# Seven block products in place of eight for the experts' down projection, with the weight sums made on VectorE

## The reference

```python
def expert_block(args):
    xb, e = args
    h = xb @ gu_w[e] + gu_b[e]
    x_glu = jnp.minimum(h[:, 0::2], SWIGLU_LIMIT)
    x_lin = jnp.clip(h[:, 1::2], -SWIGLU_LIMIT, SWIGLU_LIMIT)
    act = x_glu * jax.nn.sigmoid(SWIGLU_ALPHA * x_glu) * (x_lin + 1.0)
    return act @ dn_w[e] + dn_b[e]
```

## Time and profile before

| | |
|---|---|
| median of 3 runs | 2276.58 us (2274.15 to 2279.27) |
| the profiled execution, its own time | 2280.95 us |
| its span on the chip | 2279.3 us |
| PE busy | 2226.0 us, 98% of the span |
| DVE / ACT / POOL busy | 781.6 / 473.7 / 343.5 us |
| L2063 (gate and up), share of the chain that ended last | 39% |
| L2083 (down halves), the same | 19% |

### The profile page before, as it was taken

The page is one execution under the profiler, slowest core; times in us unless marked ns, Lnnn a source line. Parts: engine busy times, 40 slices in busy tenths (PEclk is TensorE's granted clock), DMA queues, the critical chain, the costliest instruction groups (busy, mean ns, idle before and its releaser), DMA issues.

```text
span 2279.3 us, 46156 instructions
## 1 busy us (share of the span) xinstructions
PE 2226.0 (98%) x18230; PEld 1644.5 (72%) x18231; DVE 781.6 (34%) x1853; ACT 473.7 (21%) x988; POOL 343.5 (15%) x360
## 2 busy tenths in 40 slices
PE   8999998899999999999999999999999999999997
PEld 3444445888445778887788878788778887788875
DVE  6465543455434222222222222232222232223224
ACT  3232001444333111111211111111111111111113
POOL 0000001121022212111121211122111121121112
PEclk9999999999998999999999999999999999999998
DMA  3111112334433767977777977789777988678877
GB/s 142 60 50 46 55 55 63 96 104 132 174 138 103 310 253 298 332 307 300 293 301 291 350 300 269 260 335 348 300 276 277 333 348 308 253 295 331 347 295 260
DMA packets 111411, 534.99 MB, mean 235 GB/s; under 512 B 26771, under 2 KB 60711, under 8 KB 86752
## 3 DMA queue, kind: packets, MB, share of 16 engines
q1 hardware_dynamic: 89200, 489.30, 55.2%
q0 software_dynamic: 22160, 44.98, 7.8%
HBM read 485.24 MB, written 40.05 MB: 230 GB/s over the span
## 4 chain that ended last, share of the span: by engine, by line
PE 95%; DMA 2%; DVE 1%; issue 1%; POOL 0%; ACT 0%; SPq 0%; POOLq 0%; DVEq 0%
PE ps L2063 39%; PE ps L2083 19%; PE ps L1571 9%; PE ps L1669 5%; PE ps L1942 5%; PE ps L2093 2%; PE ps L2072 2%; PE ps L1768 2%; PE ps L1618 1%; PE ps L1777 1%; PE ps L2102 1%; PE ps L1750 1%; DMA idx_g<-list_s 1%; PE ps L1782 1%; PE ps L1870 1%
## 5 line engine op out<-in xcount | busy, mean ns | idle before, releaser
L2063 PEld LDWEIGHTS ps<-arena 128*128 128x128 f32 x7808 | 925.9, 191 | 16.6 <-issue 15.1
L2063 PE MATMUL ps<-arena 128*128 128x128 f32 (+2 forms) x7808 | 926.9, 281 | 1.3 <-ACT arena L995 1.3
L2083 PE MATMUL ps<-arena 128*128 128x512 f32 x1024 | 454.3, 596 | 0.0
L2083 PEld LDWEIGHTS ps<-arena 128*128 128x128 f32 x1024 | 190.7, 190 | 221.8 <-issue 221.1
L1468 DVE TENSOR_SCALAR arena<-ps,arena 128x160 f32<-128x160 f32 x256 | 98.2, 384 | 620.1 <-PE ps L2063 536.1
L1000 ACT ACTIVATE arena<-arena 128x160 f32<-128x160 f32 x256 | 86.1, 336 | 828.3 <-DVE arena L1468 828.3
L1571 PE MATMUL ps<-arena 128*128 128x512 f32 x448 | 195.7, 594 | 0.0
L703 POOL DMA_INDIRECT sum_s<-arena,idx_s x31 | 51.5, 1663 | 824.6 <-ACT arena L1015 824.6
L1571 PEld LDWEIGHTS ps<-arena 128*128 128x128 f32 x448 | 84.5, 190 | 109.4 <-issue 109.4
L1669 PE MATMUL ps<-arena 128*128 128x512 f32 x280 | 120.6, 592 | 0.8 <-ACT arena L844 0.8
L1942 PE MATMUL ps<-arena 128*128 128x512 f32 x256 | 113.7, 594 | 0.0
(11 more groups left out here) (271 smaller groups left out, 1965.5 us busy)
## 6 DMA issues: line engine op xcount, KB each, us to landing
arena<-gu_w SPq DMA_DIRECT2D x128, 2048.0 KB, 11.7
arena<-dn_w SPq DMA_DIRECT2D x64, 2048.0 KB, 14.6
arena<-dn_b SPq DMA_DIRECT2D x32, 512.0 KB, 16.2
arena<-w_in_t SPq DMA_DIRECT2D x26, 512.0 KB, 3.2
arena<-arena SPq DMA_DIRECT2D x50, 256.0 KB, 2.7
arena<-w_out SPq DMA_DIRECT2D x2, 2048.0 KB, 8.4
arena<-x SPq DMA_DIRECT2D x8, 512.0 KB, 5.2
xn_s<-arena SPq DMA_DIRECT2D x8, 512.0 KB, 2.7
```

Source lines behind the costliest of these rows:

```text
L2063: last = nc.tensor.matmul(ps[:, f % 2, k * C:k * C + size], wslot[u][:, kt, o:o + P], xT[:, kt, 0:size], start=kt == 0, stop=kt == KT - 1, ...
L2083: last = nc.tensor.matmul(ps[:, 2 + h, :], actT[:, ft, 0:P], wslot[4 + h][:, ft, :], start=ft == 0, stop=ft == KT - 1)
```

## The change

The 128 tokens are split into two halves of 64 rows, `lower` and `upper` (as stationary operands, and as PSUM partitions), and the 1024 input features into two halves (features 0 to 3 and 4 to 7 of `actT`), so `act` becomes a11, a12 (lower rows), a21, a22 (upper rows). The weights become d11, d12 (first input half) and d21, d22. Seven products of 64 x 512 by 512 x 512 stand for the eight. `both` issues two of them side by side: one with 64 columns of the array and PSUM partitions 0 to 63, the other with the other 64. The seventh is cut into two column quarters that go side by side. DVE makes four weight sums (each 128 x 2048, in two instructions of 128 x 1024) between the steps of `glu`, and five sums of activations. DVE also puts the results together, with 64 row adds from PSUM. The down product of the last expert keeps the old form, in code of its own behind the loop. The down weights come in four loads of 1 MB, in the order of their use, at the same point of the loop as before. ACT scales the result rows in another order, at the end. The sums of rows at the end of the kernel are loaded to slots at 0 to 32 KB instead of at 112 and 56. One semaphore pair in the convolution is merged: L1271 now waits for both copies instead of one.

```diff
+                sp.dma_start(d12, down_of(e, 0, 1)).then_inc(s_wd1, 16)
+                sp.dma_start(d11, down_of(e, 0, 0)).then_inc(s_wd1, 16)
+                sp.dma_start(d22, down_of(e, 1, 1)).then_inc(s_wd22, 16)
+                sp.dma_start(d21, down_of(e, 1, 0)).then_inc(s_wd21, 16)
...
+            def down_sum(dst, a, b, op, h):
+                w = slice(h * K2 // 2, (h + 1) * K2 // 2)
+                nc.vector.tensor_tensor(dst[:, w, :], a[:, w, :], b[:, w, :], op).then_inc(s_ds, 1)
+
+            def down_sums(n, q, f):
+                if f == 2:
+                    dve.wait_ge(s_wd1, 32 * n + 32)
+                    for h in range(2):
+                        down_sum(d_dif, d12, d11, ALU.subtract, h)
+                if f in (3, 4):
+                    dve.wait_ge(s_wd22, 16 * n + 16)
+                    down_sum(d12, d12, d22, ALU.subtract, f - 3)
+                if f in (4, 5):
+                    dve.wait_ge(s_ds, 8 * q + 8 + f - 3)
+                    down_sum(d_mix, d22, d_dif, ALU.subtract, f - 4)
+                if f == 6:
+                    dve.wait_ge(s_wd21, 16 * n + 16)
+                    for h in range(2):
+                        dve.wait_ge(s_ds, 8 * q + 8 + 5 + h)
+                        down_sum(d_all, d21, d_mix, ALU.subtract, h)
...
                     for f in range(KT):
                         glu(n, e, f)
+                        down_sums(n, q, f)
+                        if f == K2:
+                            dve.wait_ge(s_act, 8 * n + KT + K2)
+                            act_sum(q, a_low, a21, a11, ALU.subtract, 0)
+                    dve.wait_ge(s_act, 8 * n + KT + KT)
+                    act_sum(q, a_sum, a21, a22, ALU.add, 1)
+                    act_sum(q, a_dif, a_sum, a11, ALU.subtract, 2)
+                    dve.wait_ge(s_db, 16 * (PIECES + 1) * (n + 1))
+                    dve.wait_ge(s_dn, o + 1)
+                    nc.vector.tensor_tensor(y_first[upper], ps[lower, 2, :], dnb[lower, 0:HALF], ALU.add).then_inc(s_ye, 1)
+                    act_sum(q, a_rest, actT[:, 0:K2, P:C], actT[:, K2:KT, P:C], ALU.add, 0)
+                    act_sum(q, a_all, a12, a_dif, ALU.subtract, 3)
                     dve.wait_ge(s_scr, n + 1)
...
+                    dve.wait_ge(s_dn, o + 2)
+                    nc.vector.tensor_tensor(Yt[upper, 0:HALF], ps[lower, 2, :], dnb[lower, 0:HALF], ALU.add).then_inc(s_ye, 1)
...
+            def both(low, high, done):
+
+                for k in range(K2):
+                    for rows, (bank, acts, weights, first) in ((lower, low), (upper, high)):
+                        width = weights.shape[-1]
+                        last = nc.tensor.matmul(ps[rows, bank, 0:width], acts[:, k, :], weights[:, k, :],
+                                                start=first and k == 0, stop=k == K2 - 1, skip_group_check=True)
+                if done:
+                    last.then_inc(s_dn, 1)
...
+            def down_first(n, q, o):
+                pe.wait_ge(s_wd1, 32 * n + 32)
+                pe.wait_ge(s_as, 5 * q + 5 + 1)
+                pe.wait_ge(s_ds, 8 * q + 8 + 4)
+                pe.wait_ge(s_ye, o + 5)
+                both((2, a11, d11, True), (3, a_low, d12, True), True)
+
+            def down_second(n, q, o):
+                pe.wait_ge(s_as, 5 * q + 5 + 3)
+                pe.wait_ge(s_ds, 8 * q + 8 + 6)
+                pe.wait_ge(s_wd21, 16 * n + 16)
+                pe.wait_ge(s_ye, o + 6)
+                both((2, a_dif, d_mix, False), (2, a12, d21, True), True)
+
+            def down_third(n, m, q, o):
+                pe.wait_ge(s_ds, 8 * q + 8 + 8)
+                pe.wait_ge(s_xe, 3 * m + 4)
+                pe.wait_ge(s_ye, o + 7)
+                both((2, a_sum, d_dif, False), (4, a22, d_all, True), True)
+                pe.wait_ge(s_as, 5 * q + 5 + 5)
+                pe.wait_ge(s_ye, o + 8)
+                both((6, a_all, d22[:, :, 0:PW], True), (6, a_all, d22[:, :, PW:HALF], True), True)
...
                     with pe.If(turn > 0):
-                        down_half(n, 0)
+                        down_first(n, q, o)
                     size = size_at(turn)
-                    transpose_tokens(m)
+                    transpose_tokens(m, 0)
+                    with pe.If(turn > 0):
+                        down_second(n, q, o)
+                    transpose_tokens(m, 1)
                     with pe.If(size > 1):
-                        down_rest(n)
+                        down_rest(n, o, q)
...
                     with pe.If(turn > 0):
-                        down_half(n, 1)
+                        down_third(n, m, q, o)
```

More of the change, by code:

```diff
@@ L241, in build @@
         wslot = [at(o, KT, HALF) for o in (0, 16, 32, 64, 80, 96)]
+        K2, TH = KT // 2, P // 2
+        d11, d21 = wslot[4][:, 0:K2, :], wslot[4][:, K2:KT, :]
+        d12, d22 = wslot[5][:, 0:K2, :], wslot[5][:, K2:KT, :]
+        d_dif, d_mix, d_all = (at(o, K2, HALF) for o in (112, 120, 128))
+        a_sum, a_dif, a_low, a_all = (at(56 + k, K2, TH) for k in range(4))
+        a_rest = at(60, K2, REST)
+        y_first, y_both = at(61, HALF), at(53, HALF)
         xg = at(48, D)
@@ L258, in build @@
         GROUPS = TT // GROUP
-        sums = [at(112 + 8 * g, GROUP, D) if g < 3 else at(56, GROUP, D) for g in range(GROUPS)]
+        sums = [at(8 * g, GROUP, D) for g in range(GROUPS)]
         rows, rows2 = at(178, D), at(182, PW)
@@ L609, in _ @@
                 pool.sem_inc(ahead, by)
-            for ahead, by in ((s_ye, 6), (s_xe, 3), (s_gd, KT), (s_act, KT)):
+            for ahead, by in ((s_ye, 5), (s_xe, 3), (s_gd, KT), (s_act, KT), (s_as, 5), (s_ds, 8)):
                 pool.sem_inc(ahead, by)
@@ new lines, in down_third, with transpose_tokens @@
+            def down_third(n, m, q, o):
[6 more added lines that the diff above has]
+                both((6, a_all, d22[:, :, 0:PW], True), (6, a_all, d22[:, :, PW:HALF], True), True)
+            def transpose_tokens(m, part):
+                if part == 0:
+                    pe.wait_ge(s_gx, 16 * m + 16)
+                for kt in range(4 * part, 4 * part + 4):
@@ L2111, in expert_pe @@
+                if part == 1:
+                    pe.wait_ge(s_gx2, 16 * m + 16)
+                    for k in range(2):
+                        last = nc.tensor.transpose(ps[:, 7, k * P:(k + 1) * P], xg2[:, k * P:(k + 1) * P], ident)
+                    last.then_inc(s_xt, 1)
             def expert_pe(r):
@@ L2141, in expert_pe @@
                         gate_up_end()
+                if isinstance(r, int):
+                    n, m = E - 1, E
+                    size = size_at(E)
+                    down_half(n, 0)
+                    for part in range(2):
+                        transpose_tokens(m, part)
+                    with pe.If(size > 1):
+                        down_rest(n, 5 * n)
+                    with pe.If(size == 1):
+                        no_rest(5 * n)
+                    down_half(n, 1)
                 if isinstance(r, int):
```

145 lines of the change are left out of this document (88 added, 57 removed).

## The result

The changed kernel took 2648.32 us (median of 4, 2644.44 to 2653.18) against 2276.18 us for the kernel before (2274.15 to 2279.27): a ratio of 1.1635 [1.1609, 1.166], 372 us slower. The forecast was 2258 us, with a range up to 2277. It was wrong by a mechanism that none of its cases held.

The account below looks back on a forecast made before the run. The prediction took PE's matmuls to bound the experts' stage. 31 turns at 0.69 us gain 21.4 us, less 3 us for first passes, is 18.4; from the median 2276.6 that gives 2258 us, range 2243 to 2277.

Parts of the forecast that it names:

- Code that runs for the first time does cost: On PE, three first passes where there were two and a separate last expert: 3 us once, bounds 0 and 8.
- Full overlap of pairs: Down product: two 64-column products run side by side, eight pairs in 3.43 us; 12.0 us a turn instead of 13.74.
- the rival of incomplete pairs: Down product: pairs overlap only partly; a quarter longer costs 93 us less the 18, about 2351 us. Chance 0.05.
- Changes of shape: PE's down part: each change of array tile shape costs 0.09 us; seven a turn where there were two.
- the load behind: PE's first weight load after a change of shape isn't hidden: 0.10 us for 128 columns, half that for 64.
- `y_first`: DVE's read of the first down product, awaited by PE before the second: 0.23 us of new waiting a turn.
- The down part: PE's down stretch of a turn: 17.93 us against 18.62 with a rest, 14.51 against 15.20 without; 0.69 us gained.
- Weight sums: DVE's eight adds of 1024 elements between `glu` steps, 1.22 us each, 9.8 us an expert: cost PE nothing.
- late DVE: Rival: DVE falls behind if an add takes 1.5 us; 0.45 us a turn lost, 2294 us. Chance 0.10.
- late weights: Down weights must land by f = 2: no wait expected; as a rival with a larger wait, slower, chance 0.02.
- DVE's last read behind the product: DVE's six adds after the last down product end some 1.8 us into the gate and up product: hidden.

Follow-up runs that it names:

- e1: The kernel before with PE's expert loop begun at slot 64 of its 256-instruction block instead of slot 1: 2569.92 us (one run) against 2278.95.
- e2: The changed kernel with all 16 matmuls of the eighth gate and up step written once, at width 160 (1757 instructions): 2273.11 us against 2278.95 before.
- e3: The kernel before with all 16 matmuls of the eighth gate and up step written once, at width 160 (1681 instructions): 2290.17 us, ratio 1.0046.
- e4: The changed kernel with DVE's weight-sum adds cut from 1024 to 16 elements, so the sums are not made: 2646.08 us (one run).
- e7: e2 with DVE's weight-sum adds cut from 1024 to 16 elements, so the sums are not made: 2273.53 us, ratio 0.9975.
- e5: The changed kernel with 12 matmuls of the eighth gate and up step shared and repeated weight waits dropped (1787 instructions): 2272.51 us, ratio 0.9972.
- e6: The changed kernel with 11 matmuls of the eighth gate and up step shared, weight waits kept (1799 instructions): 2461.07 us (one run).

## Why the prediction was wrong

**The step that failed** is "Code that runs for the first time does cost: ... I take 3 us once, bounds 0 and 8". It priced instructions that have to be fetched as something that happens on a first pass only, because in the trace of before it does happen only there. What held that true was the size and place of PE's loop, and the change alters the size: 76 more instructions. The term should have read: 1763 instructions from slot 1 leave 28 before the eighth block; the change adds 76; so every turn pays. The price by the runs is 291 us for a loop of before (e1), that is 9.4 us a turn, and 375 us for the changed kernel (2648.32 - 2273.11, against e2), 12 us a turn. The kernel itself held the warning, which I read past: it aligns its loop to a block, and it writes the end of the gate and up product once for all widths.

The Trainium skill has the mechanism and not the edge (Runtime: NRT & Kernel Launch, "Instruction fetch mechanics"): PE holds 2048 instructions, refilled in blocks of 256, and a taken branch whose target isn't in the window stands for a fetch. The traces agree with the stand, at 3.6 to 6.1 us in the median for the three branches. They differ on two points. The same section of the Trainium skill also says that the memory is only two blocks and that prefetch is purely sequential, without a cache, by which the loop of before would refetch in each turn; it didn't in 30 turns (36 packets in all). And by the 2048 instructions of the Trainium skill, eight blocks, e1 (1763 instructions over parts of eight blocks) would have fitted; it didn't. Measured here is seven blocks. That the eighth is taken by the block fetched ahead is my reading and not shown.

**The clock.** A second loss follows the first. After many of the stands PE's granted clock is low for some microseconds (not after each: behind the 3.01 us before 1720.76 the sixteen records take 3.59 us). The columns are as in the earlier trace rows, and the stretches are those of the second turn above: the first product after stands (granted 0.63, sixteen records in 5.51 us instead of 3.59), the next 8 us, the long stand, the gate and up product right behind it, and then.

```profile
1776.00:1781.90 5.90, 5.47 (x16) 1.54 (x16) 1.17 (x3) 0.00 (x0) 0.00 (x0) 0.63 0.81 319
1781.90:1790.00 8.10, 7.90 (x80) 3.83 (x82) 3.38 (x6) 1.45 (x3) 0.00 (x0) 1.00 0.01 4
...
1796.00:1806.00 10.00, 0.15 (x2) 0.00 (x0) 1.81 (x4) 2.73 (x3) 4.58 (x4) 0.74 0.87 297
1806.60:1812.00 5.40, 5.40 (x29) 5.40 (x30) 0.00 (x0) 0.00 (x0) 0.00 (x0) 0.59 1.04 320
1812.00:1829.00 17.00, 17.00 (x154) 17.00 (x154) 10.43 (x24) 1.68 (x5) 3.49 (x4) 1.00 0.78 285
```

A granted share of 0.59 is mostly the lower level, 1.2 GHz, and 1.00 the upper, 2.4 GHz. The two slow stretches here cost about 1.9 us (5.51 - 3.59) and 2.2 us (5.40 x (1 - 0.59)), on top of the stands. How much of the whole loss is of this kind can be estimated from e1, whose instructions are those of before: PE is busy 2322.1 us there and 2226.0 before, so some 96 of the 291 us are slower matmuls and the rest is stands.

**What held, read from e2, where the loop fits.**
- Full overlap of pairs: 3.59 us for eight pairs with the change of shape behind them. The prediction has 3.43 + 0.09 + 0.10 = 3.62. Confirmed; the rival of incomplete pairs is out. The prediction argued against that rival with "rows 3 and 6, at most 2% over". That holds for the rest and for L1637 once the change of shape and the load are taken off, but not for L1875 of rows 6: 0.62 us, some 0.48 without them, where full overlap is 8 x 0.054 = 0.43. The factor of 2.38 that the Trainium skill gives for three column tiles (TensorE: Matmul & The Clock Gate, "Measured speedup vs the span model") has no counterpart here with two.
- Changes of shape at 0.09 us and the load behind: 32 records of L2157 take 1785.24 - 1780.80 = 4.44 us up to the product, against 4.35 before a 128-column one in e3 (1796.02 - 1791.67). The gate and up product behind the third takes 25.12 us, against 25.01 in e3 (1791.67 - 1766.66). So 0.09 in, and 0.11 for the load on the way out, which I had at 0.10.
- `y_first`: 0.20 us of waiting before the second product, forecast 0.23; none before the third.
- The down part: 1755.68 - 1737.95 = 17.73, and with the 0.09 ahead and the 0.11 behind 17.93 us, forecast 17.93. Without a rest 14.32 + 0.20 = 14.52, forecast 14.51. From e3 to e2 a turn falls from 44.56 to 43.88 and from 50.40 to 49.72 us: 0.68, forecast 0.69.
- Weight sums, late DVE, late weights: nothing (e4, e7, and L1508's idle time of 0.0). At f = 7 DVE waits 0.42 us for PE in e2, so it isn't late. (By the prediction's own terms DVE's last read behind the product ends 0.20 + 3.3 - 1.91 = 1.6 us into the gate and up product, not 1.8; nothing hangs on it.)
- First passes were somewhat undersized even where the loop fits: 31 x 0.68 = 21.1 us of gain in the turns, but 17.1 measured between e3 and e2, 4.0 less where I had 3 (bounds 0 and 8). From one gate and up product to the next the first three turns of e2 took 59.95, 54.59 and 46.57 us, and those of e3 60.81, 53.39 and 44.56. That is 2.35 us more, where steady turns would make it 2.0 less: 4.4 us, which is what is missing.

So the sum was right to about a microsecond for the matmuls, and the change is worth 17 us to a loop that has room for it. In this kernel room costs 11 us of it (e3), and e2 ends at 6 us below before, 0.28%. That is clear of noise and very small; e2 and e5 are the only versions here that compute the whole kernel and are below the kernel before.

## What to carry to other kernels

Where an engine runs a loop, count its instructions, untaken branches and all widths included, and where it begins, as one counts SBUF: here PE keeps seven blocks of 256, and an edit that crosses the edge by more than a few slots pays 9 to 12 us in nearly every turn, whatever else it gains. In a profile the signs are packets on the instruction queue that grow with the turns, idle time put down to issue before code that wasn't changed, and branches of microseconds; the releaser named before a matmul behind such a branch is not to be trusted. An edit of a full loop is best tried first with the address of the unchanged loop moved by as many slots as the edit adds, which shows whether the edge is near.

## What the runs showed of the hardware

- Moving the unchanged loop by 63 instruction slots made the kernel 291 us slower (2278.95 to 2569.92 us).
- The edge is not a step: at eight slots over it, about 10 of 31 turns refetched, and the loss was 182 us; at 48 over (the changed kernel) and in e1 (35 over), nearly all turns did (27 to 30 of 31, by their branches over 0.5 us).
- A refetching turn fetches as many packets as the loop has blocks or somewhat more, not only the part that doesn't fit: (289 - 36) / 30 is 8.4 packets of 16 KB a turn in e1, and 9 in e6.
- Two 64-column tiles with different weights streaming 512 fp32 columns each take the time of one: 0.43 us a pair.
